# First x and first weight pieces alternately on SP's queue, the norm's factors alone on ScalarE's

## What is computed

```python
def rms_norm(x, g):
    y = x * rsqrt(mean(x * x, axis=-1) + 1e-6)
    return y * g

def even_layer(x, pre_g, w_in, ...):        # odd_layer has the same frame
    h = rms_norm(x, pre_g)
    parts = _split(h @ w_in, EVEN_IN_WIDTHS)
    ...                                     # attention and gates
    return x + rms_norm(mix @ w_out, post_g)
```

## Time and profile before

| | before |
|---|---|
| median of 3 runs | 1176.48 us (1176.21 to 1177.12) |
| the profiled execution's own time | 1176.14 us |
| its span, first to last instruction | 1174.2 us |
| PE busy | 1163.3 us, 99% of the span |
| DVE busy | 736.7 us, 63% |
| ACT busy | 584.1 us, 50% |
| mean granted clock of PE | 0.997 |

### The profile page before, as it was taken

One profiled execution on the slowest core, in us unless ns is written; L12 is line 12 of the kernel. 1 busy time (PEld: TensorE's weight loads), 2 busy tenths in 40 slices (PEclk: granted clock), 3 DMA queues, 4 the chain that ended last, 5 costly groups with the idle time before them and its releaser, 6 DMA issues.

```text
span 1174.2 us, 14646 instructions
## 1 busy us (share of the span) xinstructions
PE 1163.3 (99%) x5476; PEld 972.2 (83%) x5476; DVE 736.7 (63%) x845; ACT 584.1 (50%) x748; POOL 102.9 (9%) x147
## 2 busy tenths in 40 slices
PE   9999999999999999999999999999999999999997
PEld 7888888888888888788888888888888888888886
DVE  6686565666665975754665555565746667668654
ACT  6645454445555654564545444444444444446442
POOL 1000001000000310010100101102011002002100
PEclk9999999999999999999999999999999999999999
DMA  9866676744745784455767666666765656455741
GB/s 360 283 208 222 202 242 198 234 164 143 253 163 229 185 264 179 172 191 181 257 198 238 212 213 217 212 218 203 246 202 177 244 187 229 144 183 179 260 149 72
DMA packets 85816, 244.03 MB, mean 208 GB/s; under 512 B 33264, under 2 KB 50832, under 8 KB 60672
## 3 DMA queue, kind: packets, MB, share of 16 engines
q1 hardware_dynamic: 82416, 234.92, 59.7%
q0 software_dynamic: 2624, 7.75, 1.9%
q10 hardware_dynamic: 720, 0.61, 0.2%
HBM read 220.17 MB, written 8.39 MB: 195 GB/s over the span
## 4 chain that ended last, share of the span: by engine, by line
PE 97%; DVE 1%; ACT 1%; DMA 1%; issue 0%; ACTq 0%; DVEq 0%
PE acc L506 89%; PE bank_x L669 2%; PE bank_y L622 1%; PE bank_x L665 1%; PE bank_y L611 1%; PE bank_x L653 1%; DMA resid<-x_turned 1%; PE bank_y L638 0%; PE bank_x L638 0%; PE bank_y L618 0%; DVE w_lo L1087 0%; DVE mix L1343 0%; PE acc L533 0%; DVE resid L1398 0%; PE acc L539 0%
## 5 line engine op out<-in xcount | busy, mean ns | idle before, releaser
L506 PE MATMUL acc<-w_hi,act_hi 128*128 128x512 f32 x1560 | 615.2, 394 | 0.6 <-DVE w_lo L1087 0.6
L506 PE MATMUL acc<-w_lo,act_hi 128*128 128x512 f32 x1560 | 608.0, 390 | 0.0
L1087 DVE TENSOR_TENSOR w_lo<-raw,w_hi 128x2048 fp32r<-128x2048 f32 x192 | 442.4, 2307 | 176.9 <-ACT w_hi L778 176.7
L778 ACT ACTIVATE w_hi<-raw 128x2048 fp32r<-128x2048 f32 x192 | 367.9, 1916 | 293.3 <-PE acc L506 284.0
L506 PE MATMUL acc<-w_hi,act_lo 128*128 128x512 f32 x1560 | 417.5, 389 | 0.0
L506 PEld LDWEIGHTS acc<-w_hi,act_lo 128*128 128x128 f32 x1560 | 292.8, 188 | 61.9 <-DVE act_lo L1105 0.4
L506 PEld LDWEIGHTS acc<-w_hi,act_hi 128*128 128x128 f32 x1560 | 293.2, 188 | 58.5 <-DVE w_lo L1087 1.1
L506 PEld LDWEIGHTS acc<-w_lo,act_hi 128*128 128x128 f32 x1560 | 293.2, 188 | 57.1
L785 ACT ACTIVATE unit<-acc,pre_r 128x512 f32<-128x512 f32 x78 | 49.5, 686 | 125.4 <-PE acc L506 122.2
L443 POOL TENSOR_TENSOR rope_c<-unit,cst 128x256 f32<-128x256 f32 (+1 forms) x19 | 14.1, 742 | 747.7 <-ACT unit L785 596.1
L1246 DVE TENSOR_SCALAR mix<-bank_x 128x256 f32<-128x256 f32 (+1 forms) x24 | 10.1, 423 | 65.7 <-PE bank_x L669 65.7
(11 more groups left out here) (181 smaller groups left out, 616.5 us busy)
## 6 DMA issues: line engine op xcount, KB each, us to landing
raw<-weights SPq DMA_DIRECT2D x192, 1024.0 KB, 5.0
qk_raw<-postg SPq DMA_DIRECT2D x176, 64.0 KB, 2.0
p_moved<-p_blocks SPq DMA_DIRECT2D x16, 256.0 KB, 5.6
probs<-p_moved SPq DMA_DIRECT2D x64, 64.0 KB, 1.9
raw<-weights SPq DMA_DIRECT2D x7, 512.0 KB, 9.3
postg<-post_g POOLq DMA_DIRECT2D x2, 1024.0 KB, 8.2
resid<-x_perm POOLq DMA_DIRECT2D x2, 1024.0 KB, 8.8
p_moved<-p_blocks SPq DMA_DIRECT2D x16, 128.0 KB, 5.0
```

The lines of the kernel that those rows point to most:

```text
L506: m = nc.tensor.matmul(tiles[t][:, :], a[:, kt, t * P:(t + 1) * P], w[:, buf, kk * NB:(kk + 1) * NB], start=(kt == 0 and a is act_hi and w ...
L778: nc.scalar.activation(w_hi[:, at % SPLIT, :], raw[:, at % RAW, :], ACT.Copy).then_inc(S["hi_ready"], 1)
L1087: nc.vector.tensor_tensor(w_lo[:, at % SPLIT, :], raw[:, at % RAW, :], w_hi[:, at % SPLIT, :].bitcast(F32), ALU.subtract).then_inc(S["lo_r ...
```

## The change

SP's program issues six transfers where it issued three: x block 0, weight block 0, x block 1, weight block 1, x blocks 2 to 3, weight blocks 2 to 3. ACT's program issues only the factors; its three x transfers are gone. All semaphores and all waits keep their names and counts.

```diff
-            for n, cols in enumerate(PIECES):
+            for n, (cols, k) in enumerate(zip(PIECES, (slice(0, 1), slice(1, 2), slice(2, 4)))):
+                sp.dma_start(xT[:, k, :], x_turned[:, k, :]).then_inc(x_first[n], 16)
                 sp.dma_start(raw[:, 0, cols], weights[0][:, cols]).then_inc((w_first + landed)[n], 16)
...
-            act.dma_start(xT[:, 0, :], x_turned[:, 0, :]).then_inc(x_first[0], 16)
             act.dma_start(preg[:, :, :], pre_g).then_inc(S["preg_in"], 16)
             act.wait_ge(S["o_full"], CREDIT)
             nc.scalar.activation(warm[:, :], credit[:, 0:1], ACT.Copy)
-            for kt in (1,):
-                act.dma_start(xT[:, kt, :], x_turned[:, kt, :]).then_inc(x_first[kt], 16)
-            act.dma_start(xT[:, 2:4, :], x_turned[:, 2:4, :]).then_inc(x_first[2], 16)
             act.wait_ge(S["preg_in"], 16)
```

## The result

| | before | after |
|---|---|---|
| median | 1176.37 us (12 runs, 1175.71 to 1178.14) | 1177.93 us (12 runs, 1177.11 to 1179.56) |
| ratio to before, 95% interval | | 1.0015, 1.0008 to 1.0022 |
| the profiled execution's own time, and its span | 1176.14, 1174.2 us | 1179.56, 1177.7 us |
| PE busy | 1163.3 us | 1164.7 us |
| mean granted clock | 0.997 | 0.996 |

The change makes the kernel a little slower, by 0.15%: inside the widest range and inside "no difference over 0.2%" (the interval reaches 0.22%), but 1.3 us above the forecast and above the forecast's own range, which ended at 1177.3. The profiled execution is the slowest of the twelve, so its parts are larger than those of the median.

A forecast was written before the change was run, and what follows sets the result against it. PE's own work bounds the kernel, with PE held at line 557 by DVE and chunk 5's landing. -1.7 at the start, +1.7 at line 557 and +0.1 from the stream gave a median of 1176.6 us, range 1176.1 to 1177.3.

The forecast's parts named there:

- the widest range: Whole time, range over all cases: down to 1175.2, up to 1178.6 us.
- no difference over 0.2%: Whole time: within 0.2% (2.4 us) of the kernel before, at a chance of 0.93.
- What bounds the kernel: 97% of the span is PE's work; at line 557 PE waits 0.26 us for DVE, which hangs on chunk 5's landing.
- The factors and x block 0: Start: factors, moved to ACT's first slot, land at 5.0 to 5.65 us where they landed at 6.11.
- Chunk 0's last piece at 7.9: Start: weight blocks 2 to 3 land at 7.9 us where they landed at 7.5.
- chunk 1's second half "at 11.5 again": Start: same bytes ahead on both queues, so it lands at 11.5 us as before; ACT waits about 1.1 for it.
- issues are covered as long as bytes are queued: Transfer stream: three more SP issues, 0.45 us each, 1.35 in all, are nearly all hidden by queued bytes.
- the gain of 1.7 at the start: Chunk 1's first products (line 506) begin at 13.5 where the chain has 15.32; PE ahead by 1.7 us.
- The shift of the stream: Whole transfer stream: +0.1 us, between bounds of -0.3 and +1.35.
- The rival in which the stream follows SP's issues: Chunks 5 and 6 land up to 1.35 us late and line 557 with them: 1177.8 us, chance 0.08.
- the picture that the forecast drew: PE early at chunk 1, resting 1.5 to 2.2 us before line 557, which begins within 0.4 of 42.78; chance 0.52.
- The rival of the clock: Behind a 2.0 us rest at line 557 PE's clock falls to half for about 3.4 us, costing 1.7: 1178.3, chance 0.30.

The follow-up runs named there:

- x0_on_sp: Kernel before, with x block 0 alone moved first onto SP's queue; factors first on ScalarE's queue, x block 1 and x blocks 2 to 3 behind them; ratio 1.0007.
- three_small_issues: Kernel before, with three 16 KB copies of the factors that nobody reads issued on SP, one ahead of each first weight piece; ratio 1.0019.
- weights_held: Kernel before, with SP's first three weight issues held by waits on DVE fills to 1.32, 2.20 and 3.07 us, no transfer added; ratio 1.0015.
- weights_then_x: Changed kernel with its six SP transfers reordered: x block 0, three weight pieces, x block 1, x blocks 2 to 3; ratio to before 1.0005.
- after_sums_later: Changed kernel with the one-column sums ahead of chunk 7 in place of chunk 6; median 1176.48 us, ratio to before 1.0001.
- factors_first: Kernel before, with the factors issued ahead of x block 0 and the x pieces still on ScalarE's queue; ratio 0.9996.
- x_on_pool: Kernel before, with the three x pieces on GpSimd's queue and the factors alone on ScalarE's; ratio 0.9999.

## Why the prediction was right or wrong

- *What bounds the kernel: right.* The sums wait for DVE and DVE for the landing of chunk 5, in the changed kernel as before: chunk 5's split moved by 1.82 and the sums by 1.78. x0_on_sp shows an early PE resting there.
- *The factors and x block 0: right in direction, too small.* Taken at 5.0 to 5.65, the first act_hi began at 3.17. The factors landed 2.4 us after issue, where 4.9 had been carried over from the second slot.
- *Chunk 0's last piece at 7.9, chunk 1's second half "at 11.5 again": wrong.* They came at 10.0 (3.10 + 6.9) and 14.43. The step that failed is the one before them, that issues are covered as long as bytes are queued. The text named a condition (the engines running dry in the first 2 us); they ran short later, at 0.80 from 3.5 to 7. So the gain of 1.7 at the start never arose: chunk 1 began at 16.36, not at 13.5.
- *The shift of the stream: wrong in size.* It was taken at +0.1 between -0.3 and +1.35, and was 1.8, outside both bounds. The rival in which the stream follows SP's issues came nearest, with 1177.8 at a chance of 0.08. But the runs show that it is the issue of chunk 0's second and third piece that counts (1.22 to 1.78 for 1.39 to 1.42), and not the number of issues or those behind the pieces.
- *Luck in the time.* The missing gain cost nothing only because PE would have rested at the sums anyway: its lateness of 1.04 at chunk 1 still left a rest of 0.72 there. The time lies inside the range because the range had been drawn up to 1178.6 for a fall of the clock or a late stream alone; the picture that the forecast drew did not come.
- *The rival of the clock: came true in the profiled execution*, at its price of 1.7 us. But the rest that it was argued from, 2.0 us, did not come. The clock fell behind a rest of 0.72 in the changed kernel and of 0.71 in three_small_issues, and did not fall behind 0.72 in weights_held (1.00 from 45.5 to 48.9) or 1.71 in x0_on_sp (1.00 from 44.4 to 47.8), each with the 1.47 us of one-column products. These are single executions; others of the last two kernels took up to 1180.88 and 1179.69, at a mean clock of 0.995. The length of the rest alone doesn't decide it; what does is open.
- *The page.* The Trainium skill, "DMA: Bandwidth & Descriptors", section "Issuing engines are not separate DMA queues", has a second queue save only the issuing sequencer's time and calls that time usually small. The runs agree with the first half (six transfers on one queue cost nothing measurable in weights_then_x, 1.0005), and disagree on the weight of the second: here issues of 0.43 us each cost 0.15% to 0.19% where they stand between the large pieces.

What stays open is why less is moved for so long. SP had issued 2.3 MB by 4.8 us in the changed kernel, and 0.9 MB had moved by 5.7 (4.7 us at 194 GB/s), so bytes were queued while engines stood idle. Idleness is also only a part: a share of 0.80 in place of 0.97 would leave 282 of the 342 GB/s, and 223 were moved. None of the runs looks into a single engine's queue. That the sums come 0.5 later in the changed kernel than with held weights needs no cause of its own: the changed kernel's start, run again in after_sums_later, had chunk 5 at 29.77, as the held ones have.

## What to carry to other kernels

While the transfers of a start are building up, keep the large ones on an issuing engine back to back, and put small ones behind them or on another engine: three issues of 16 KB between the pieces cost as much as the whole change, and nothing measurable behind them. Before counting an earlier start, look for the next point at which PE meets another engine, even where the chain names no releaser: 0.26 us of "issue" hid a chain through DVE back to a landing. And where PE has to rest early, look at the work that waits and at the rest itself: moving the sums and filling the first rest together gave the only time here that is clearly below the kernel before (0.9989). Neither alone is shown to gain: moving the sums gave 0.9995 (0.9986 to 1.0004), and filling the rest was not run by itself.

## What was not expected of the hardware

How long a first transfer takes at the start hangs on what else is issued at that moment, and not on its own slot alone. The 16 KB of factors landed 2.4 us after issue from the first slot of ScalarE's queue with x block 0 first on SP's, and 3.5 and 3.4 from the same slot in factors_first and x_on_pool, where a weight piece of 256 KB stood first there. From the second slot they took 4.9 before, and 2.9 in weights_held, where the first weight piece was issued 0.56 later. x block 0 goes the same way from one first slot, that of ScalarE's queue: 4.1 before, 2.1 in weights_held. Here are x block 0 and the factors before, in KB and us to landing, and then both in the changed kernel:

```profile
resid<-x_turned ACTq DMA_DIRECT2D x1, 128.0 KB, 4.1
preg<-pre_g ACTq DMA_DIRECT2D x1, 16.0 KB, 4.9
...
resid<-x_turned SPq DMA_DIRECT2D x1, 128.0 KB, 2.2
preg<-pre_g ACTq DMA_DIRECT2D x1, 16.0 KB, 2.4
```

And the first landings of one start differ by up to 1 us from one execution to the next (7.26 and 8.06, 11.79 and 12.80 above), so a start read from one trace is a sample, not the rule.
